# VectorE's order in three places: low parts in the early expert steps and the gate blocks, and the rotation tables of the projections

## What is computed

```python
z = rms_norm(x, lw['g_mix']) @ lw['w_in']            # then split: u, q, kc, vc, ks, vs, kw, vw, gates
q = rope_partial(rms_norm(q.reshape(bsz, t, N_HEADS, HEAD_DIM), lw['g_q']), pos)
...
xr, xi = lax.associative_scan(...)                    # a complex diagonal state space, 64 states per group
...
s = jnp.einsum('nhsd,hskd->nhsk', q, subkeys)         # PEER: two times 128 keys per head, 16 best of the pairs
...
act = jax.nn.gelu(jnp.einsum('chkd,cd->chk', u_tab[ec], xc))
out = jnp.einsum('chk,chkd->cd', gc * act, v_tab[ec]) # 8 heads x 16 experts a token, of 16384 single-neuron experts
```

## Time and profile before

| | |
|---|---|
| median of 3 runs (lowest, highest) | 2677.67 us (2671.87, 2681.81) |
| the profiled execution | 2674.46 us |
| its span, first to last instruction | 2672.8 us |
| PE busy | 2316.9 us, 87% of the span |
| DVE busy | 1792.6 us, 67% |
| ACT, POOL busy | 767.0, 764.3 us, 29% each |
| granted TensorE clock, mean | 0.913 |
| DMA | 448.25 MB, 168 GB/s over the span |

### The profile page before, as it was taken

The page is one execution under the profiler, slowest core; times in us unless marked ns, Lnnn a source line. Parts: engine busy times, 40 slices in busy tenths (PEclk is TensorE's granted clock), DMA queues, the critical chain, the costliest instruction groups (busy, mean ns, idle before and its releaser), DMA issues. The chain is left out here.

```text
span 2672.8 us, 36866 instructions
## 1 busy us (share of the span) xinstructions
PE 2316.9 (87%) x11591; PEld 1995.8 (75%) x11591; DVE 1792.6 (67%) x4092; ACT 767.0 (29%) x1366; POOL 764.3 (29%) x667
## 2 busy tenths in 40 slices
PE   7784698886669999998499778898999999999989
PEld 5453588553458899987488767788889999999968
DVE  6834301664322209999899878888888889889862
ACT  1031111342122223342344332222223323323331
POOL 1320220200113234443255412222243333334312
PEclk9887797788789899998799889999999999999999
DMA  5105441500332124442456657666788788888630
GB/s 200 11 28 119 161 126 63 160 1 6 93 97 79 56 87 136 147 143 88 163 176 183 178 213 263 241 242 247 266 324 282 279 299 281 282 290 294 232 138 36
DMA packets 194123, 448.25 MB, mean 168 GB/s; under 512 B 26401, under 2 KB 109602, under 8 KB 184610
## 3 DMA queue, kind: packets, MB, share of 16 engines
q1 hardware_dynamic: 140082, 222.74, 25.7%
q0 software_dynamic: 44288, 156.92, 17.0%
q10 hardware_dynamic: 9648, 67.24, 6.5%
HBM read 394.07 MB, written 54.80 MB: 168 GB/s over the span
## 5 line engine op out<-in xcount | busy, mean ns | idle before, releaser
L2465 PE MATMUL e_ps<-w_hi,v_hi 128*128 128x448 f32 x1024 | 389.7, 381 | 51.0 <-DVE w_lo L2361 41.5
L2465 PE MATMUL e_ps<-w_lo,v_hi 128*128 128x448 f32 x1024 | 386.9, 378 | 0.0
L2465 PE MATMUL e_ps<-w_hi,v_lo 128*128 128x448 f32 x1024 | 386.2, 377 | 0.0
L2465 PEld LDWEIGHTS e_ps<-w_hi,v_hi 128*128 128x128 f32 x1024 | 200.2, 195 | 76.3 <-DVE v_lo L2300 53.6
L2465 PEld LDWEIGHTS e_ps<-w_lo,v_hi 128*128 128x128 f32 x1024 | 200.3, 196 | 19.3
L2465 PEld LDWEIGHTS e_ps<-w_hi,v_lo 128*128 128x128 f32 x1024 | 199.7, 195 | 19.9
L1446 PE MATMUL e_ps<-x_hi,u_hi 128*128 128x448 f32 x512 | 189.6, 370 | 17.8 <-DVE u_lo L2296 17.8
L2300 DVE TENSOR_TENSOR v_lo<-v_raw,v_hi 128x512 fp32r<-128x512 f32 x256 | 175.4, 687 | 30.6 <-ACT v_hi L2200 29.2
L2306 DVE TENSOR_TENSOR hT<-hT,e_ps 128x448 f32<-128x448 f32 x256 | 157.6, 616 | 56.5 <-PE e_ps L2465 56.5
L1446 PE MATMUL e_ps<-x_lo,u_hi 128*128 128x448 f32 x512 | 189.5, 370 | 0.0
L1446 PE MATMUL e_ps<-x_hi,u_lo 128*128 128x448 f32 x512 | 189.3, 370 | 0.0
(11 more groups left out here) (489 smaller groups left out, 5196.5 us busy)
## 6 DMA issues: line engine op xcount, KB each, us to landing
v_raw<-in_v_tab ACTq DMA_DIRECT2D x62, 1024.0 KB
u_raw<-in_u_tab SPq DMA_DIRECT2D x64, 512.0 KB
gate_scr<-gate_stage SPq DMA_DIRECT2D x14, 2048.0 KB, 9.2
mixT<-gate_scr SPq DMA_DIRECT2D x32, 896.0 KB
r_u_raw<-in_u_tab SPq DMA_DIRECT2D x50, 512.0 KB, 3.9
gelu_scr<-mixT SPq DMA_DIRECT2D x32, 448.0 KB, 2.7
acts_and_rows<-gelu_scr SPq DMA_DIRECT2D x16, 896.0 KB, 8.9
m_w_raw<-in_w_mix SPq DMA_DIRECT2D x24, 512.0 KB, 3.5
```

The costliest lines, as they stand in the source:

```text
L2465: mm = nc.tensor.matmul(ps[:, 4 + c % 4, 0:TD], as_r(v[:, c % 4, e]), as_r(w[:, b, e]), start=(e == 0 and n == 0), stop=(e == EG - 1 and n ...
```

## The change

It moves VectorE's instructions in three places, and one subtraction per gate block from GpSimd to VectorE. No other engine's order changes, but for the missing subtraction on GpSimd.

```diff
-            for i in range(5):
-                double(i)
-            for t in range(TILES):
-                if t == 1:
-                    double(5)
+            def rows(t):
                 m, b = TILE_ROWS[t], t % 2
                 dve.wait_ge(hsq_ready, 3 * t + 3)
...
                 nc.vector.tensor_tensor(qk3[:, :, 0:16], ra[0:m], rb[0:m], ALU.add).then_inc(rows_ready, 1)
+
+            for i in range(3):
+                double(i)
+            for t in range(TILES):
+                rows(t)
+                if t < 3:
+                    double(3 + t)
...
                     nc.vector.tensor_copy(first_picks[:, b], k.idxT[:, 0, bass.ds(2 * TB * i + TB * b, TB)]).then_inc(picks_copied, 1)
+                    dve.wait_ge(u_hi_made, 2 * i + (b + 1))
+                    nc.vector.tensor_tensor(as_r(u_lo[:, b]), u_raw[:, b], u_hi[:, b], ALU.subtract).then_inc(u_lo_made, 1)
                     for n in range(TB):
...
             def blocks(i):
                 for b in range(2):
-                    pool.wait_ge(u_hi_made, 2 * i + (b + 1))
-                    nc.gpsimd.tensor_tensor(as_r(u_lo[:, b]), u_raw[:, b], u_hi[:, b], ALU.subtract).then_inc(u_lo_made, 1)
-
                     pool.wait_ge(picks_copied, 2 * i + (b + 1))
...
                     for c in (2 * e, 2 * e + 1):
                         add(s - 1, c)
+                        if c % 2 == 0:
+                            w_low(s, b, e)
+                        elif e == 0:
+                            if first:
+                                weigh(0, 0, EARLY)
+                                for j in range(EARLY):
+                                    accumulate_first(j)
+                            dot(s, 0)
+                        elif e == 1:
+                            dot(s, 1)
+                        else:
+                            if e == 2:
+                                weigh(s, EARLY * s, EARLY)
+                            accumulate(s, e - 2, EARLY * s)
                         if c < 4:
                             v_low(s - 1, c + 4)
                         else:
                             v_low(s, c - 4)
-                        if c % 2 == 0:
-                            w_low(s, b, e)
-                    if first and e == 0:
-                        weigh(0, 0, EARLY)
-                        for j in range(EARLY):
-                            accumulate_first(j)
-                    if e < 2:
-                        dot(s, e)
-                    if e == 2:
-                        weigh(s, EARLY * s, EARLY)
-                    if e >= 2:
-                        accumulate(s, e - 2, EARLY * s)
```

## The result

The changed kernel takes **2600.59 us** (median of 4 runs, 2590.85 to 2608.77) where the kernel before takes 2679.74 (4 runs, 2671.87 to 2685.39): a ratio of 0.9705, 95% interval 0.9662 to 0.9749. Forecast were 2598 and a range of 2581 to 2630. The profiled execution of the changed kernel took 2590.85 us (span 2589.1), that of before 2674.46.

A forecast was written before the change was run, and what follows sets the result against it. Early steps were bound by a wait going round between engines (TensorE held for w_lo), gate blocks by VectorE, projections by TensorE's wait for first rows. Gains 53 + 18 + 9 = 80 us gave 2598 us, range 2581 to 2630.

The forecast's parts named there:

- forecast 53 us from a step of 20.7: Early steps: step falls from 24.33 to 20.7 us, 51 us over 14 steps, plus 2 us in the first step.
- The short chain of an expert: Early steps: VectorE's own chain for one expert takes 3.92 us where it was 4.40.
- the prediction's estimate was 1.7: Early steps: 1.7 us of TensorE's work lost per step to the low clock.
- the first rival: Early steps: clock still falls in every step; at a step of 21.8 the gain is 37 us, 2614 us; chance 0.17.
- just fits: Early steps: a gathered row's latency of 8.7 us fits the about 9.0 us VectorE leaves it.
- the lower bound: Early steps: cost of waiting for gathered rows, lower bound 0, upper 2.6 us a step; 0 taken.
- The distance forecast as 9.0 us: Early steps: VectorE's time between an accumulation's end and the next dot, 11.55 us before the change.
- forecast 18 us from 14.45 a block: Gate blocks: new block 14.45 us, 1.3 us gained in each of 14, 18 us, ends 12 and 24.
- the choice nearer the upper bound: Gate blocks: gain 0.86 us a block if low-clock blocks stay, 1.42 if they go; 1.3 taken.
- u_lo against GpSimd, forecast 0: Gate blocks: u_lo is issued before GpSimd's one-hots, cost 0; rival order costs 1.47 us a block, 2616 us, chance 0.07.
- forecast 8.8 us: Projections: two doublings move behind the first rows, so TensorE restarts 8.8 us earlier; ends 7 and 10.5.

The follow-up runs named there:

- the repeated w_raw: Changed kernel with the fourth expert's w_raw made three times in each of 14 early steps; 2636.55 us, 0.9858 to the kernel before.
- The halves: Kernel before with one half of the early steps' edit each: w_lo ahead of v_lo, 0.9802; extra piece moved with w_lo left behind v_lo, 0.9982.
- again: Changed kernel run once more, unedited, beside the kernel before (the second comparison): 2607.91 us, ratio 0.9750.
- projections alone: Kernel before with only the new order of the projections; 2664.20 us, 0.9972.
- combined: All three edits, but extra pieces left at the expert's end, u_lo behind the first token's one-hots, 6 more one-hots a block on GpSimd; 2578.70 us, 0.9645 to before.
- early steps alone: Kernel before with only the new order of the early expert steps, w_lo and extra piece both moved; 2620.99 us, 0.9807.
- gate blocks alone: Kernel before with only the gate blocks' u_lo made by VectorE alone; 2651.74 us, 0.9930.
- half of the early edit: Kernel before with w_lo ahead of the first v_lo, the extra piece left at the expert's end; 2619.86 us, 0.9802.
- u_lo behind the one-hots: Changed kernel with VectorE's u_lo in the gate blocks behind the first token's two one-hots; 2601.36 us, 0.9722 to the kernel before.
- more one-hots: Changed kernel with the third token's first one-hot made by GpSimd in quads 1 to 6 of a gate block; 2587.03 us, 0.9678 to before.
- the halved dots: Changed kernel with dots and accumulations of the early steps on 512 of 1024 columns; 2579.58 us, 0.9638 to the kernel before.

## Why the prediction was right, point by point

- **Early steps, forecast 53 us from a step of 20.7.** Run alone: 50. In the two profiles, from the first w_raw (1562.1 and 1537.6) to TensorE's restart in step 16 (1948.51 and 1874.01): 386.4 and 336.4, again 50 (47 in the changed kernel's second profile). The starts, of the changed kernel's w_raw and of TensorE's restarts before and after:

```profile
L2372 DVE TENSOR_TENSOR w_raw<-acts_and_rows,mixT x60: 943/959/981, 1537.6 to 1851.4; 128x448 f32<-128x448 f32 x60
1948.51 0.47 PE L2465 MATMUL e_ps<-w_hi,v_hi 128*128 128x448 f32 x1 [3.35 <-DVE v_lo L2300]
1874.01 0.47 PE L2469 MATMUL e_ps<-w_hi,v_hi 128*128 128x448 f32 x1 [3.12 <-DVE v_lo L2302]
```

  The mean step is 20.8 in the profile; without its first, which ran at 0.92 behind the hold of 3.63, it is 20.74, as forecast. The short chain of an expert, v_hi being ready, a hold near 1 us and the full clock are all in the rows. The run with the repeated w_raw puts the clock's share of the step's gain of 3.5 us at some 1.1 (the prediction's estimate was 1.7), and it shows that a hold of 2.4 to 2.6 us in each step is enough for the low clock of the first rival.
- **What the prediction did not separate**: it summed the edit of the extra pieces with that of w_lo. The halves show that w_lo's place brings everything. The extra piece's brings 0 to 10 us when alone, by its interval, and in the profiles it costs 4 to 6 us in company: from the first w_raw to the restart in step 16 it is 332.7 us with w_lo's move alone and 336.4 to 339.0 in three profiles with both. The run times of the two (0.9807 and 0.9802) don't tell them apart. Of the 4 to 6, 1.3 to 2.3 lie in TensorE's first step, which ran partly at the low clock in these three (21.9 to 22.9 us) and not with w_lo's move alone (20.6). Why the rows come later in that order, though VectorE's distance from the end of an accumulation to the dot is 8.9 us in both, isn't settled.
- **Gathered rows, forecast "just fits", cost 0.** 2.6 us in all over 30 dots (4.1 in the second profile), 1.5 of it in one dot of the last early step: right at the lower bound, with a margin as small as put. The distance forecast as 9.0 us is 8.9.
- **Gate blocks, forecast 18 us from 14.45 a block.** Run alone 19.5; in the profiles 17.8 (from the first copy to the experts' first copy on VectorE: 228.2 and 210.4). The block is 14.37. The low clock of some blocks went for most of them, as the choice nearer the upper bound assumed.
- **u_lo against GpSimd, forecast 0.** Right in its sum, since the one-hots that stood are needed only with the fourth token. Its reason, that u_lo is issued first, isn't shown to decide: with its recorded start 0.09 us behind the one-hot's, u_lo kept its length as well. The Trainium skill ("SBUF — State Buffer", "Who interferes with whom") says that whoever issues first has the ports for the whole instruction; the recorded starts in these traces don't show such an order. In the kernel before, 8 of the 13 one-hots that stood started 0.01 us ahead of GpSimd's subtraction and 5 some 0.06 behind it; one of the 8:

```profile
1318.01 2.46 DVE L1965 TENSOR_SCALAR one_hot<-iota,idx_T 128x128 f32<-128x128 f32 x1
1318.02 2.36 POOL L1973 TENSOR_TENSOR g_u_lo<-g_u_raw,g_u_hi 128x1024 fp32r<-128x1024 f32 x1
```

  What all the traces have in common is another thing: the subtraction keeps its length (2.36 us on GpSimd, 1.21 on VectorE) and the one-hot stands, whichever engine has which. Whether that is a rule isn't settled; which of the two stands is not read from the recorded starts.
- **Projections, forecast 8.8 us.** Here the size was off downstream. Times from the start of the third doubling, means of four profiles with the new order (after, again, projections alone, combined) and four without (before, early steps alone, gate blocks alone, half of the early edit):

| up to | without | with | gained |
|---|---|---|---|
| the last rows of the projections | 78.3 | 69.0 | 9.3 |
| the first clearing of q_heads | 540.3 | 532.5 | 7.7 |
| the last clearing of the selected-page scores | 672.7 | 666.3 | 6.4 |
| the first copy of the gate blocks | 1209.6 | 1204.7 | 4.9 |

  The 8.8 arrive where they were forecast and fade on the way; over all 13 profiles the four gains are 9.0, 7.5, 6.2 and 5.2. Single profiles of one order differ by up to 10 us at the last of these points, so of the loss between 9 and 5 us only the direction is shown, and not which waits swallow it. Alone, the edit measured 7 us.
- **The sum.** Forecast 53 + 18 + 9 = 80; run one by one 50 + 19.5 + 7 = 77, each with an interval of 7 or 8 us either way. The profiled pair differs by 83.7 us of span, of which 9.2 lie in the late steps (724.3 and 715.1 us from step 16 to the end), where nothing was edited. They aren't the change's, as the last section shows; without them the pair gives 74.5. So the mechanisms and the sizes of the parts came out within some 6 us, but that the medians' 79 lies so near the forecast 80 is partly luck: the second comparison gave 66.

## What to carry to other kernels

When an engine stands for a piece that is late because something ahead of it on another engine waits for a third, moving that piece ahead of the waiting one can pay twice, as here: the wait goes, and with it the hold that lowered TensorE's clock. Price such an order by adding up the instructions of the engine that sets the pace, and then check what comes next (here TensorE at 19.5 us a step). An operation that runs free on an idle engine is not free if it stops another: 1.2 us of its work on the full engine was cheaper than the 2.1 us that the full engine stood for it (2.38 where 0.29 was needed).

## What the runs showed of the hardware that was not expected

TensorE's products have two paces at the full clock. In 150 us of uninterrupted products of the late steps, at a granted clock of 1.00, the traces hold 742 or 728 of them, that is one in 202 or 206 ns. Windows of the changed kernel and of the same kernel again, one fence each:

```profile
1976.00:2126.00 150.00, 150.00 (x742) 139.00 (x741) 130.76 (x182) 47.95 (x80) 56.25 (x47) 1.00 0.84 297
```

```profile
1990.00:2140.00 150.00, 150.00 (x728) 136.25 (x727) 128.65 (x178) 45.96 (x77) 59.51 (x47) 1.00 0.84 296
```

The two are one program. Of 13 profiles 8 had the closer pace in the late steps (after, the early edit whole and in both halves, the projections' edit, the repeated w_raw, u_lo behind the one-hots, more one-hots) and 5 the wider (before, again, the gate blocks' edit, the combined version, the halved dots). It isn't a property of an execution either. In the early steps, where TensorE is held once a step, both paces stand next to each other. The first and the last start of the 96 products of two steps in succession of the changed kernel are 19.70 and 19.33 us apart:

```profile
1624.49 0.44 PE L2469 MATMUL e_ps<-w_hi,v_hi 128*128 128x448 f32 x1 [0.92 <-DVE w_lo L2363]
1644.19 0.37 PE L2469 MATMUL e_ps<-w_hi,v_lo 128*128 128x448 f32 x1
1645.39 0.44 PE L2469 MATMUL e_ps<-w_hi,v_hi 128*128 128x448 f32 x1 [0.84 <-DVE w_lo L2363]
1664.72 0.37 PE L2469 MATMUL e_ps<-w_hi,v_lo 128*128 128x448 f32 x1
```

Over the expert products of all 13 profiles, 208 of the 209 stretches of over 40 products between two waits of over 0.1 us keep one pace throughout, 202.7 or 206.7 ns from start to start, and some four in ten stretches have another than the one before. The late steps are a single stretch of some 600 us, so one restart fixes some 12 us of an execution, as much as the scatter of the runs. What picks the pace at a restart is open; the granted clock doesn't show it. A profile pair of this kernel must therefore be compared stage by stage, and a difference in the late steps isn't laid to an edit elsewhere.

The other two were met above: TensorE held for 2.4 to 2.6 us in every step showed 0.93, held for 0.5 to 1.3 us 1.00; and of VectorE's u_lo and GpSimd's one-hots it was the one-hots that stood, whichever started first in the records.
